# A mixer's decay table and one-hot rows, zero-filled from 48 to 128 rows

## The chip, the cores and the metric

The kernel runs on one core of a Trainium2 chip (trn2). The metric is the device time of one execution in microseconds. The time before is the median of three runs.

## The reference, cut to what matters

One layer of a hybrid network over 128 context tokens and 2,048 latent tokens of width 1,024, in chunks of 128 tokens. The part that the change touches is the decay between two tokens of one chunk in the state-space scan, for 8 heads and two directions:

```python
def ssd_chunked_scan(x, dt, a, bm, cm, h0):
    ...
    a_cum = jnp.cumsum((dt * a).reshape(b, nc, CHUNK, G, R), axis=2)
    ...
    lower = jnp.tril(jnp.ones((CHUNK, CHUNK), bool))[None, None, :, :, None, None]
    seg = a_cum[:, :, :, None] - a_cum[:, :, None, :]
    decay_in = jnp.exp(jnp.where(lower, seg, -jnp.inf))
    cb = jnp.einsum('bclgn,bcsgn->bclsg', cc, bc)
    y_diag = jnp.einsum('bclsgr,bcsgrp->bclgrp', cb[..., None] * decay_in, X)
```

Around it stand norms, the input projection, a depthwise convolution, pooling, the output projection, an expert-choice feed-forward layer with 16 experts, and a last norm.

## The kernel before

Tokens are split into 17 tiles of 128 (`NT` = 17; the first is the context). The program is a row of stages, each a block in which all engines have their own instruction stream, with a barrier at its end: `front` (input projection, convolution, pooling), `decays`, `back_states`, `mixer`, `selection`, `experts`, `final`.

`decays` makes the table of step sizes and cumulated decays `tab`, and a second copy of the cumulated decays, turned so that tokens lie along the columns: `acum_t`, 48 rows by 2,176 bf16 columns. Its 48 rows (`N3`) are 16 (8 heads in two directions, `HH`) times 3: an f32 value is split into three bf16 parts (`stack`, lines 1058 to 1062). VectorE does the softplus in a chain of dependent operations (lines 1032 to 1048), TensorE sums over tokens (1011 to 1013), VectorE splits, TensorE turns (1019), and ScalarE copies the result into `acum_t` (998, 999). Beside it GpSimd fills and selects constants (966 to 978): the triangles of minus infinity `negf` and `negb`, a bf16 identity, and `pick`, 48 rows by 16 x 128 columns, which holds for each of the 16 heads-and-directions ones in the three rows of that head. The selects wait for all fills (line 970).

`mixer` reads both. For each tile, `decay_rows` (TensorE) builds four quads of masks, two by two, in two PSUM banks `b34`. A quad is one product of the identity with a triangle over 512 columns (line 1351, all 128 rows) and, added on top, four products of `pick` with the tile's columns of `acum_t` (line 1354, 48 rows, 128 columns each). ScalarE takes the exponential of each quad (1517), VectorE adds the two directions (1609) and multiplies with the chunk's C-B products (1616), and TensorE's `scan` multiplies with the tokens (1385). The order of TensorE's work is written out by hand: for tile i `scan`, `route` of tile i-3 (1463), quads 0 and 1 of tile i+1, `turn_rows` (1453), half a projection of tile i-1 (`project`, 1441, 24 products), `turn_rows` again, quads 2 and 3 of tile i+1, `turn` of tile i+1 (1364 to 1375), the other half of the projection, `turn_y` (1425). Each step waits on counters of the engines that feed it.

Inputs of products that have to be exact are split in two f32r parts; their weight loads have 128 rows and 128 columns. The experts' stage gathers tokens in blocks of 128, 128 and 16 rows (`L2087` turns them).

Of the kernel before, what the change touches and what calls it, by code (L numbers as in the profile page):

```python
# [24 lines left out]
BF16 = mybir.dt.bfloat16  # L25
# [3 lines left out]
ACT = mybir.ActivationFunctionType  # L29
AX_X = mybir.AxisListType.X  # L30

P = 128
# [3 lines left out]
T = CTX + LAT  # L36
# [5 lines left out]
HH = 2 * H  # L42
# [13 lines left out]
R_DTB, R_ALOG, R_DSKIP, R_EDGE = 0, 16, 32, 40  # L56
# [884 lines left out]
def decays(nc, g, io):  # L941

    with ExitStack() as ctx:
# [7 lines left out]
        ps_row = k.ps("ps_row", [P, 2, D])  # L951
        made = k.sem("masks_made")
        dch = k.sem("decay_chain")
        mag_done, exp_done, aexp_done = k.sem("mag_done"), k.sem("spexp_done"), k.sem("aexp_done")
        lndt_done = k.sem("lndt_done")
        da_done, sums_done, acum_done, exps_done = k.sem("da_done"), k.sem("sums_done"), k.sem("acum_done"), k.sem("exps_done")
        row_done, row_copied = k.sem("row_done"), k.sem("row_copied")
        stack_done, acum_turned = k.sem("stack_done"), k.sem("acum_turned")
        tab = g.tab
        rows = [(g.mod[:, G_A:G_A + 8, w], g.ga_rows[:, w, :]) for w in range(2)]  # L960
# [3 lines left out]
        @block.gpsimd  # L964
        def _(pool):
            pool.memset(g.negf[:, :], 0.0).then_inc(made, 1)
            pool.memset(g.negb[:, :], 0.0).then_inc(made, 1)
            pool.tensor_copy(g.identb[:, :], g.ident[:, :]).then_inc(made, 1)
            pool.memset(g.pick[:, :, :], 0.0).then_inc(made, 1)
            pool.wait_ge(made, 4)  # L970

            pool.affine_select(out=g.negf[:, :], in_=g.negf[:, :], compare_op=ALU.is_ge, fill=NEG, base=0,
                               pattern=[[1, P]], channel_multiplier=-1)
            pool.affine_select(out=g.negb[:, :], in_=g.negb[:, :], compare_op=ALU.is_ge, fill=NEG, base=0,
                               pattern=[[-1, P]], channel_multiplier=1)
            for n in range(3):
                pool.affine_select(out=g.pick[:, :, :], in_=g.pick[:, :, :], compare_op=ALU.not_equal, fill=1.0,
                                   base=-HH * n, pattern=[[-1, HH], [0, P]], channel_multiplier=1).then_inc(made, 1)
                pool.wait_ge(made, 5 + n)

        @block.scalar
        def _(act):
            act.preload_act_table_set("natural_log_exp_and_others")
            act.activation(aexp[:, :], g.rows[:, R_ALOG:R_ALOG + HH], ACT.Exp).then_inc(aexp_done, 1)
            act.wait_ge(mag_done, 1)
            act.activation(e[:, :, :], mag[:, :, :], ACT.Exp, scale=-1.0).then_inc(exp_done, 1)
            for n, (_, dst) in enumerate(rows):
                act.wait_ge(row_done, n + 1)
                act.activation(dst, ps_row[:, n % 2, :], ACT.Copy).then_inc(row_copied, 1)
            act.wait_ge(da_done, 1)  # L990
            act.activation(z[:, :, :], tab[:, :, T_DT:T_DT + HH], ACT.Ln).then_inc(lndt_done, 1)
            act.wait_ge(acum_done, 1)

            act.activation(tab[:, :, T_EACUM:T_EACUM + HH], v[:, :, :], ACT.Exp).then_inc(exps_done, 1)
            act.activation(mag[:, :, :], mag[:, :, :], ACT.Exp).then_inc(exps_done, 1)
            act.activation(tab[:, :, T_DEC:T_DEC + HH], ps_tot[:, :, :], ACT.Exp).then_inc(exps_done, 1)
            act.wait_ge(acum_turned, 1)
            act.activation(g.acum_t[:, 0:T - P], ps_acum[0:N3, 0:T - P], ACT.Copy)
            act.activation(g.acum_t[:, T - P:T], ps_f[0:N3, :, :].rearrange("p t h -> p (t h)")[:, 0:P], ACT.Copy)

        @block.tensor
        def _(pe):
            for n, (col, _) in enumerate(rows):
                if n >= 2:
                    pe.wait_ge(row_copied, n - 1)
                for kk in range(KD):
                    mm = pe.matmul(ps_row[:, n % 2, P * kk:P * kk + P], col[:, kk:kk + 1].broadcast_to([P, P]),
                                   g.ident[:, :], start=True, stop=True)
                mm.then_inc(row_done, 1)
            pe.wait_ge(da_done, 1)  # L1010
            pe.matmul(ps_f[:, :, :], g.tri_le[:, :], tab[:, :, T_DA:T_DA + H], start=True, stop=True)
            pe.matmul(ps_b[:, :, :], g.tri_ge[:, :], tab[:, :, T_DA + H:T_DA + HH], start=True, stop=True)
            pe.matmul(ps_tot[:, :, :], g.ones[:, :], tab[:, :, T_DA:T_DA + HH], start=True, stop=True).then_inc(sums_done, 1)
            pe.wait_ge(made, 3)
            pe.wait_ge(row_copied, 2)
            pe.wait_ge(stack_done, 1)
            for i in range(NT):
                out = ps_acum[0:N3, P * i:P * i + P] if i < NT - 1 else ps_f[0:N3, :, :].rearrange("p t h -> p (t h)")[:, 0:P]
                mm = pe.matmul(out, stack[:, i, :], g.identb[:, :], start=True, stop=True)
            mm.then_inc(acum_turned, 1)  # L1020

        @block.vector
        def _(dve):
            count = [0]

            def link(ins):
                count[0] += 1
                ins.then_inc(dch, 1)
                dve.wait_ge(dch, count[0])

            bias = g.rows[:, R_DTB:R_DTB + HH].unsqueeze(1).broadcast_to([P, NT, HH])
            link(dve.tensor_tensor(v[:, :, :], g.dt_raw[:, :, :], bias, ALU.add))
            dve.scalar_tensor_tensor(mag[:, :, :], v[:, :, :], -1.0, v[:, :, :], ALU.mult, ALU.max).then_inc(mag_done, 1)
            link(dve.tensor_scalar(relu[:, :, :], v[:, :, :], 0.0, None, ALU.max))
            dve.wait_ge(exp_done, 1)

            link(dve.tensor_scalar(z2[:, :, :], e[:, :, :], 2.0, None, ALU.add))
            link(dve.reciprocal(poly[:, :, :], z2[:, :, :]))
            link(dve.tensor_tensor(z[:, :, :], e[:, :, :], poly[:, :, :], ALU.mult))
            link(dve.tensor_tensor(z2[:, :, :], z[:, :, :], z[:, :, :], ALU.mult))  # L1040
            link(dve.tensor_scalar(poly[:, :, :], z2[:, :, :], 1.0 / 17, None, ALU.mult))
            for n in (15, 13, 11, 9, 7, 5, 3):
                link(dve.scalar_tensor_tensor(poly[:, :, :], poly[:, :, :], 1.0 / n, z2[:, :, :], ALU.add, ALU.mult))
            link(dve.scalar_tensor_tensor(poly[:, :, :], poly[:, :, :], 1.0, z[:, :, :], ALU.add, ALU.mult))
            link(dve.scalar_tensor_tensor(tab[:, :, T_DT:T_DT + HH], poly[:, :, :], 2.0, relu[:, :, :], ALU.mult, ALU.add))
            dve.wait_ge(aexp_done, 1)
            aneg = aexp[:, :].unsqueeze(1).broadcast_to([P, NT, HH])
            dve.scalar_tensor_tensor(tab[:, :, T_DA:T_DA + HH], tab[:, :, T_DT:T_DT + HH], -1.0, aneg,
                                     ALU.mult, ALU.mult).then_inc(da_done, 1)
            dve.wait_ge(da_done, 1)  # L1050
            dve.wait_ge(sums_done, 1)
            dve.tensor_copy(v[:, :, 0:H], ps_f[:, :, :])
            link(dve.tensor_copy(v[:, :, H:HH], ps_b[:, :, :]))
            dve.wait_ge(lndt_done, 1)
            dve.tensor_tensor(mag[:, :, :], ps_tot[:, :, :], v[:, :, :], ALU.subtract).then_inc(acum_done, 1)
            dve.tensor_tensor(tab[:, :, T_NACUM:T_NACUM + HH], z[:, :, :], v[:, :, :], ALU.subtract)

            link(dve.tensor_copy(stack[:, :, 0:HH], v[:, :, :]))
            link(dve.tensor_tensor(rest[:, :, :], v[:, :, :], stack[:, :, 0:HH], ALU.subtract))
            link(dve.tensor_copy(stack[:, :, HH:2 * HH], rest[:, :, :]))  # L1060
            link(dve.tensor_tensor(rest[:, :, :], rest[:, :, :], stack[:, :, HH:2 * HH], ALU.subtract))
            dve.tensor_copy(stack[:, :, 2 * HH:N3], rest[:, :, :]).then_inc(stack_done, 1)
            dve.wait_ge(exps_done, 2)
            dve.tensor_tensor(tab[:, :, T_WEND:T_WEND + HH], mag[:, :, :], tab[:, :, T_DT:T_DT + HH], ALU.mult)


# [1345 lines left out]
def build(nc, io):  # L2412
    Kit.used.clear()
    with ExitStack() as ctx:
# [17 lines left out]
        with ExitStack() as part:  # L2432
# [2 lines left out]
            g.negf, g.negb = kk.sb("negf", [P, P], BF16), kk.sb("negb", [P, P], BF16)  # L2435
            g.identb = kk.sb("identb", [P, P], BF16)
            g.ga_rows = kk.sb("ga_rows", [P, 2, D])
            g.pick, g.acum_t = kk.sb("pick", [N3, HH, P], BF16), kk.sb("acum_t", [N3, T], BF16)
            g.wohi, g.wolo = kk.sb("wohi", [P, KD, D], F32R), kk.sb("wolo", [P, KD, D], F32R)
            g.wrs = kk.sb("wrs", [P, 2, KD, STRIP])  # L2440
            g.hf = kk.sb("hf", [P, 2, 512])
# [54 lines left out]
```

## Time and profile before

| | before |
|---|---|
| median of the runs | 2522.24 us |
| runs | 2519.30, 2522.86, 2522.24 us |
| the profiled execution | 2521.52 us |
| its span, first to last instruction | 2519.9 us |
| granted TensorE clock, mean | 0.938 |
| TensorE busy | 2261.8 us, 90% |
| VectorE busy | 1381.2 us, 55% |
| ScalarE busy | 998.2 us, 40% |
| GpSimd busy | 238.3 us, 9% |

One execution is profiled; the times of single instructions come from it. PE is TensorE's products, PEld its weight loads, DVE VectorE, ACT ScalarE, POOL GpSimd. The granted clock is a share of full speed: 1.00 is the level of 2.4 GHz and 0.50 that of 1.2 GHz. A product's recorded length is from its start to the end of its last column, and products overlap, so the distance between two starts says what one costs in a row of them, not its length.

### The profile page before, as it was taken

To read this page: it belongs to the slowest core of one execution; us is meant where nothing else is said; L and a number is where in the kernel's file an instruction comes from. 1 tells how busy PE (TensorE), PEld (TensorE's weight loads), DVE (VectorE), ACT (ScalarE), POOL (GpSimd) and SP (SyncE) were. 2 spreads that over 40 slices of the span, in tenths; PEclk is the share of its full clock that TensorE was granted. 3 is DMA by queue.
4 is the path that set the end of the run, shared out by engine and by line. 5 is a ranking of instruction groups with operands and counts; after the bars stand their busy time and mean duration, and the time that the engine had idled before them with its cause. 6 is when DMAs were issued, how large, how long until landed. Compare 5 with 4: busy or idle time off the path is not lost. (4 is left out here: it accounts for less than half of the span.)

```text
span 2519.9 us, 40046 instructions
## 1 busy us (share of the span) xinstructions
PE 2261.8 (90%) x15772; PEld 2052.0 (81%) x15772; DVE 1381.2 (55%) x2184; ACT 998.2 (40%) x1734; POOL 238.3 (9%) x307
## 2 busy tenths in 40 slices
PE   4999999956799999629999999999999999999980
PEld 2878887855688887518999999999999999999980
DVE  2655443226477777464566456655565555645543
ACT  3642222222455554104444444444444344434424
POOL 0000000021111111000100111101010110011010
PEclk8999999987799999758999999999999999999995
DMA  8533442216344443033665565656565655556537
GB/s 277 180 114 120 144 144 96 88 60 223 91 138 138 139 139 117 34 118 103 192 195 167 176 193 177 200 160 187 176 209 154 183 181 188 173 176 188 176 94 285
DMA packets 318699, 396.57 MB, mean 157 GB/s; under 512 B 12014, under 2 KB 273150, under 8 KB 316558
## 3 DMA queue, kind: packets, MB, share of 16 engines
q1 hardware_dynamic: 287406, 287.67, 35.7%
q0 software_dynamic: 22400, 86.06, 11.7%
q10 hardware_dynamic: 8800, 21.56, 2.3%
q8 instruction: 62, 1.02, 0.2%
q14 instruction: 31, 0.25, 0.0%
HBM read 318.12 MB, written 77.14 MB: 157 GB/s over the span
## 5 line engine op out<-in xcount | busy, mean ns | idle before, releaser
L2227 DVE TENSOR_TENSOR experts_wlo<-experts_raw,experts_whi 128x2048 fp32r<-128x2048 f32 x192 | 439.9, 2291 | 421.8 <-ACT experts_whi L2171 421.8
L2109 PE MATMUL experts_ps_r<-experts_xhi,experts_whi 128*128 128x272 f32 x2048 | 605.2, 296 | 5.4 <-DVE experts_xlo L2281 5.4
L2109 PE MATMUL experts_ps_r<-experts_xhi,experts_wlo 128*128 128x272 f32 x2048 | 593.8, 290 | 0.0
L2109 PE MATMUL experts_ps_r<-experts_xlo,experts_whi 128*128 128x272 f32 x2048 | 590.5, 288 | 0.0
L2109 PEld LDWEIGHTS experts_ps_r<-experts_xhi,experts_whi 128*128 128x128 f32 x2048 | 386.1, 189 | 8.5 <-DVE experts_xlo L2281 5.5
L2109 PEld LDWEIGHTS experts_ps_r<-experts_xlo,experts_whi 128*128 128x128 f32 x2048 | 386.9, 189 | 0.0
L2109 PEld LDWEIGHTS experts_ps_r<-experts_xhi,experts_wlo 128*128 128x128 f32 x2048 | 386.1, 189 | 0.0
L2171 ACT ACTIVATE experts_whi<-experts_raw 128x2048 fp32r<-128x2048 f32 x192 | 366.1, 1907 | 14.6 <-DMA experts_raw<-in_w_gate 13.8
L2109 PE MATMUL experts_ps_r<-experts_hhi,experts_whi 128*128 128x272 f32 x1024 | 299.6, 293 | 0.2 <-DVE experts_hlo L2301 0.2
L2109 PE MATMUL experts_ps_r<-experts_hhi,experts_wlo 128*128 128x272 f32 x1024 | 296.3, 289 | 0.0
L2109 PE MATMUL experts_ps_r<-experts_hlo,experts_whi 128*128 128x272 f32 x1024 | 294.8, 288 | 0.0
L521 PE MATMUL front_ps<-front_hhi,front_whi 128*128 128x384 f32 (+1 forms) x640 | 236.1, 369 | 0.0
L521 PE MATMUL front_ps<-front_hhi,front_wlo 128*128 128x384 f32 (+1 forms) x640 | 230.8, 361 | 0.0
L521 PE MATMUL front_ps<-front_hlo,front_whi 128*128 128x384 f32 (+1 forms) x640 | 230.8, 361 | 0.0
L2195 ACT ACTIVATE experts_hhi<-experts_hid 128x272 fp32r<-128x272 f32 x128 | 55.2, 431 | 353.9 <-DVE experts_hid L2298 353.9
L2109 PEld LDWEIGHTS experts_ps_r<-experts_hhi,experts_whi 128*128 128x128 f32 x1024 | 192.7, 188 | 1.1 <-DVE experts_hlo L2301 0.5
L2109 PEld LDWEIGHTS experts_ps_r<-experts_hlo,experts_whi 128*128 128x128 f32 x1024 | 193.0, 188 | 0.0
L2109 PEld LDWEIGHTS experts_ps_r<-experts_hhi,experts_wlo 128*128 128x128 f32 x1024 | 192.6, 188 | 0.0
L521 PEld LDWEIGHTS front_ps<-front_hhi,front_whi 128*128 128x128 f32 x640 | 120.8, 189 | 25.4 <-ACT front_u L659 12.6
L659 ACT ACTIVATE front_u<-front_ps 128x128 f32<-128x128 f32 (+2 forms) x90 | 40.2, 469 | 248.9 <-PE front_ps L521 227.9
L2049 POOL DMA_INDIRECT x<-experts_yo,experts_idx x48 | 72.1, 1502 | 684.1 <-DVE experts_yo L2288 521.1
L2190 ACT ACTIVATE experts_sg<-experts_ps_r 128x272 f32<-128x272 f32 x128 | 51.0, 398 | 214.9 <-PE experts_ps_r L2109 214.9
(393 smaller groups left out, 3453.5 us busy)
## 6 DMA issues: line engine op xcount, KB each, us to landing
experts_raw<-in_w_gate SPq DMA_DIRECT2D x64, 1024.0 KB, 5.0
experts_raw<-in_w_up SPq DMA_DIRECT2D x64, 1024.0 KB, 5.0
experts_raw<-in_w_down SPq DMA_DIRECT2D x64, 1024.0 KB, 5.3
shared_whalf<-in_w_ada SPq DMA_DIRECT2D x16, 1024.0 KB, 5.2
mixer_mz<-mixed SPq DMA_DIRECT2D x17, 768.0 KB, 7.9
mixed<-front_acc POOLq DMA_DIRECT2D x9, 1024.0 KB, 4.2
resid<-early_xin POOLq DMA_DIRECT2D x17, 512.0 KB, 3.7
mixer_xs<-resid SPq DMA_DIRECT2D x17, 512.0 KB, 4.0
```

Source lines behind the costliest of these rows:

```text
L521: mm = pe.matmul(ps[:, out, 0:n], wt[buf][:, kk, :], h[:, kk, t0:t0 + n], start=(kk == 0 and q == 0), stop=(kk == KD - 1 and q == 2))
L659: ins = act.activation(dst_u[:, uo:uo + pn], ps[:, bank_of(s), po:po + pn], func)
L2049: pool.indirect_dma_start(io["x2"], bass.IndirectOffsetOnAxis(idx[2][0:n, a:a + 1], 0), yo[0:n, a, :], None, compute_op=ALU.add).then_inc( ...
L2109: mm = pe.matmul(dst, w[:, c % RING, kk, cols], r[:, kk, :], start=(kk == 0 and q == 0), stop=(kk == KD - 1 and q == 2))
L2171: act.activation(whi[:, c % RING, :, :], raw[:, c % RAW, :, :], ACT.Copy).then_inc(whi_done, 1)
L2190: act.activation(sg[:, ft % 2, :], ps_r[:, (2 * ft) % 4, 0:ROWS], ACT.Silu).then_inc(silu_done, 1)
L2195: act.activation(hhi[:, ft, :], hid[:, ft % 2, :], ACT.Copy).then_inc(hhi_done, 1)
L2227: dve.tensor_tensor(wlo[:, c % RING, :, :], raw[:, c % RAW, :, :], whi[:, c % RING, :, :].bitcast(F32), ALU.subtract).then_inc(wlo_done, 1)
```

## The change

`pick` and `acum_t` get 128 rows instead of 48. Rows 48 to 127 hold zeros: `pick`'s come from its fill, which now covers 128 rows, and `acum_t` gets a fill of its own on GpSimd, as the fifth, so that all thresholds of `made` behind it move by one. The products of line 1354 then read 128 rows of both; no line of the mixer changes. ScalarE's copies into `acum_t` are confined to rows 0 to 47 and wait for the fill. Five semaphores that ScalarE raised (`exp_done`, `aexp_done`, `lndt_done`, `exps_done`, `row_copied`) become one counter, `scalar_done`, on which the others wait with thresholds, and a branch that was never taken goes.

```diff
-        mag_done, exp_done, aexp_done = k.sem("mag_done"), k.sem("spexp_done"), k.sem("aexp_done")
-        lndt_done = k.sem("lndt_done")
...
+        mag_done, scalar_done = k.sem("mag_done"), k.sem("scalar_done")
+        A_RATE, A_EXP, A_ROWS, A_LN, A_DECAYS = 1, 2, 4, 5, 7
...
             pool.memset(g.pick[:, :, :], 0.0).then_inc(made, 1)
-            pool.wait_ge(made, 4)
+            pool.memset(g.acum_t[:, :], 0.0).then_inc(made, 1)
+            pool.wait_ge(made, 5)
...
-                pool.wait_ge(made, 5 + n)
+                pool.wait_ge(made, 6 + n)
...
-            act.activation(aexp[:, :], g.rows[:, R_ALOG:R_ALOG + HH], ACT.Exp).then_inc(aexp_done, 1)
+            act.activation(aexp[:, :], g.rows[:, R_ALOG:R_ALOG + HH], ACT.Exp).then_inc(scalar_done, 1)
...
+            act.wait_ge(made, 5)
             act.wait_ge(acum_turned, 1)
-            act.activation(g.acum_t[:, 0:T - P], ps_acum[0:N3, 0:T - P], ACT.Copy)
-            act.activation(g.acum_t[:, T - P:T], ps_f[0:N3, :, :].rearrange("p t h -> p (t h)")[:, 0:P], ACT.Copy)
+            act.activation(g.acum_t[0:N3, 0:T - P], ps_acum[0:N3, 0:T - P], ACT.Copy)
+            act.activation(g.acum_t[0:N3, T - P:T], ps_f[0:N3, :, :].rearrange("p t h -> p (t h)")[:, 0:P], ACT.Copy)
...
             pe.wait_ge(made, 3)
-            pe.wait_ge(row_copied, 2)
+            pe.wait_ge(scalar_done, A_ROWS)
...
-            dve.wait_ge(exp_done, 1)
+            dve.wait_ge(scalar_done, A_EXP)
...
-            dve.wait_ge(aexp_done, 1)
+            dve.wait_ge(scalar_done, A_RATE)
...
-            dve.wait_ge(lndt_done, 1)
+            dve.wait_ge(scalar_done, A_LN)
...
-            dve.wait_ge(exps_done, 2)
+            dve.wait_ge(scalar_done, A_DECAYS)
...
-            g.pick, g.acum_t = kk.sb("pick", [N3, HH, P], BF16), kk.sb("acum_t", [N3, T], BF16)
+            g.pick, g.acum_t = kk.sb("pick", [P, HH, P], BF16), kk.sb("acum_t", [P, T], BF16)
```

## Rows read from the trace of the kernel before

**Rows 1.** The page: granted TensorE clock in 40 equal slices, in tenths.

```profile
PEclk8999999987799999758999999999999999999995
```

**Rows 2.** Stretches: length, busy us (instructions) by engine, granted clock, DMA share, GB/s.

```profile
660.00:680.00 20.00, 16.55 (x68) 13.85 (x69) 11.70 (x19) 9.96 (x33) 3.09 (x3) 0.60 0.14 40
...
691.76:992.96 301.20, 301.20 (x1919) 241.94 (x1918) 221.82 (x365) 160.56 (x503) 38.11 (x42) 1.00 0.42 135
```

**Rows 3.** TensorE's products in order of time: start, length in us, line, out<-in.

```profile
781.80 0.64 PE L1463 MATMUL mixer_b<-mixer_h2t,ssd_wrs 128*32 128x128 f32 x16
782.37 0.39 PE L1351 MATMUL mixer_b<-ssd_negf,ssd_identb 128*128 128x512 bf16 x1
782.70 0.39 PE L1354 MATMUL mixer_b<-ssd_acum_t,ssd_pick 48*128 48x128 bf16 x4
783.02 0.39 PE L1351 MATMUL mixer_b<-ssd_negf,ssd_identb 128*128 128x512 bf16 x1
...
783.67 0.66 PE L1453 MATMUL mixer_b<-kept_ident,mixer_xr 128*128 128x128 f32 x4
...
789.64 0.60 PE L1453 MATMUL mixer_b<-kept_ident,mixer_xr 128*128 128x128 f32 x4
790.08 0.38 PE L1351 MATMUL mixer_b<-ssd_negb,ssd_identb 128*128 128x512 bf16 x1
...
792.88 0.48 PE L1441 MATMUL mixer_b<-ssd_wohi,mixer_mhi 128*128 128x512 f32 x1
...
798.90 1.90 PE L1385 MATMUL mixer_b<-mixer_xt,mixer_ex 128*128 128x64 f32 x16
```

**Rows 4.** TensorE's weight loads in order of time, with the idle time before.

```profile
782.69 0.22 PEld L1354 LDWEIGHTS mixer_b<-ssd_acum_t,ssd_pick 48*128 48x128 bf16 x4 [0.23 <-issue]
...
789.97 0.10 PEld L1351 LDWEIGHTS mixer_b<-ssd_negb,ssd_identb 128*128 128x128 bf16 x1
```

**Rows 5.** Groups, 691.76 to 992.96: count | busy us, mean ns | idle before.

```profile
L1354 PE MATMUL mixer_b<-ssd_acum_t,ssd_pick 48*128 48x128 bf16 x224 | 22.1, 219 | 0.0
...
L1354 PEld LDWEIGHTS mixer_b<-ssd_acum_t,ssd_pick 48*128 48x128 bf16 x224 | 12.4, 94 | 14.2 <-issue 14.2
```

**Rows 6.** Groups of weight loads in the experts, 1300 to 1420, by shape.

```profile
L2087 PEld LDWEIGHTS experts_ps_x<-kept_ident,experts_xg 128*128 128x128 f32 x24 | 2.9, 141 | 0.7 <-issue 0.7
...
L2087 PEld LDWEIGHTS experts_ps_x<-kept_ident,experts_xg 16*128 16x128 f32 x12 | 1.6, 133 | 2.0 <-issue 2.0
```

**Rows 7.** VectorE in order of time, in the same tile.

```profile
778.35 1.23 DVE L1695 TENSOR_TENSOR mixer_xr<-mixer_o,mixer_xs 128x1024 f32<-128x1024 f32 x1
...
790.28 0.69 DVE L1672 COPY mixer_h2t<-mixer_b 128x512 f32<-128x512 f32 x1 [1.84 <-PE mixer_b L1453]
...
795.68 1.21 DVE L1616 TENSOR_TENSOR mixer_ex<-mixer_ex,mixer_cbt 128x1024 f32<-128x1024 f32 x1
```

**Rows 8.** GpSimd in order of time, decays and the start of the next stage.

```profile
539.71 1.79 POOL L969 MEMSET ssd_pick<- 48x2048 bf16 x1
...
542.20 6.32 POOL L977 TENSOR_SCALAR_AFFINE_SELECT ssd_pick<-ssd_pick 48x2048 bf16<-48x2048 bf16 x3
563.84 0.53 POOL L1102 MEMSET ssd_wrs<- 128x512 f32 x1 [15.32 <-SPq L1118]
```

**Rows 9.** VectorE in order of time, decays.

```profile
540.00 1.66 DVE L1034 TENSOR_SCALAR decays_sp_relu<-decays_sp_v 128x272 f32<-128x272 f32 x1
541.70 0.40 DVE L1037 TENSOR_SCALAR decays_sp_z<-decays_sp_e 128x272 f32<-128x272 f32 x1
...
546.69 1.98 DVE L1041 TENSOR_SCALAR decays_sp_poly<-decays_sp_z 128x272 f32<-128x272 f32 x1
548.71 3.30 DVE L1043 SCALAR_TENSOR_TENSOR decays_sp_poly<-decays_sp_poly,decays_sp_z 128x272 f32<-128x272 f32 x7
```

**Rows 10.** ScalarE in order of time, end of decays.

```profile
561.50 1.87 ACT L998 ACTIVATE ssd_acum_t<-decays_ps_row 48x2048 bf16<-48x2048 f32 x1 [3.68 <-PE decays_ps_f L1019]
```

**Rows 11.** TensorE's products in order of time, before the experts' first tile.

```profile
1113.25 1.02 PE L2075 MATMUL experts_ps_i<-experts_val_e,experts_onehot 128*128 128x5 bf16 x32 [5.24 <-DVE experts_onehot L2239]
```

More of the change, by code:

```diff
@@ L953, in decays @@
         dch = k.sem("decay_chain")
-        mag_done, exp_done, aexp_done = k.sem("mag_done"), k.sem("spexp_done"), k.sem("aexp_done")
-        lndt_done = k.sem("lndt_done")
-        da_done, sums_done, acum_done, exps_done = k.sem("da_done"), k.sem("sums_done"), k.sem("acum_done"), k.sem("exps_done")
-        row_done, row_copied = k.sem("row_done"), k.sem("row_copied")
+        mag_done, scalar_done = k.sem("mag_done"), k.sem("scalar_done")
+        A_RATE, A_EXP, A_ROWS, A_LN, A_DECAYS = 1, 2, 4, 5, 7
+        da_done, sums_done, acum_done = k.sem("da_done"), k.sem("sums_done"), k.sem("acum_done")
+        row_done = k.sem("row_done")
         stack_done, acum_turned = k.sem("stack_done"), k.sem("acum_turned")
@@ L983, in _ @@
             act.preload_act_table_set("natural_log_exp_and_others")
-            act.activation(aexp[:, :], g.rows[:, R_ALOG:R_ALOG + HH], ACT.Exp).then_inc(aexp_done, 1)
+            act.activation(aexp[:, :], g.rows[:, R_ALOG:R_ALOG + HH], ACT.Exp).then_inc(scalar_done, 1)
             act.wait_ge(mag_done, 1)
-            act.activation(e[:, :, :], mag[:, :, :], ACT.Exp, scale=-1.0).then_inc(exp_done, 1)
+            act.activation(e[:, :, :], mag[:, :, :], ACT.Exp, scale=-1.0).then_inc(scalar_done, 1)
             for n, (_, dst) in enumerate(rows):
                 act.wait_ge(row_done, n + 1)
-                act.activation(dst, ps_row[:, n % 2, :], ACT.Copy).then_inc(row_copied, 1)
+                act.activation(dst, ps_row[:, n % 2, :], ACT.Copy).then_inc(scalar_done, 1)
             act.wait_ge(da_done, 1)
-            act.activation(z[:, :, :], tab[:, :, T_DT:T_DT + HH], ACT.Ln).then_inc(lndt_done, 1)
+            act.activation(z[:, :, :], tab[:, :, T_DT:T_DT + HH], ACT.Ln).then_inc(scalar_done, 1)
             act.wait_ge(acum_done, 1)
-            act.activation(tab[:, :, T_EACUM:T_EACUM + HH], v[:, :, :], ACT.Exp).then_inc(exps_done, 1)
-            act.activation(mag[:, :, :], mag[:, :, :], ACT.Exp).then_inc(exps_done, 1)
-            act.activation(tab[:, :, T_DEC:T_DEC + HH], ps_tot[:, :, :], ACT.Exp).then_inc(exps_done, 1)
+            act.activation(tab[:, :, T_EACUM:T_EACUM + HH], v[:, :, :], ACT.Exp).then_inc(scalar_done, 1)
+            act.activation(mag[:, :, :], mag[:, :, :], ACT.Exp).then_inc(scalar_done, 1)
+            act.activation(tab[:, :, T_DEC:T_DEC + HH], ps_tot[:, :, :], ACT.Exp).then_inc(scalar_done, 1)
+            act.wait_ge(made, 5)
             act.wait_ge(acum_turned, 1)
-            act.activation(g.acum_t[:, 0:T - P], ps_acum[0:N3, 0:T - P], ACT.Copy)
-            act.activation(g.acum_t[:, T - P:T], ps_f[0:N3, :, :].rearrange("p t h -> p (t h)")[:, 0:P], ACT.Copy)
+            act.activation(g.acum_t[0:N3, 0:T - P], ps_acum[0:N3, 0:T - P], ACT.Copy)
+            act.activation(g.acum_t[0:N3, T - P:T], ps_f[0:N3, :, :].rearrange("p t h -> p (t h)")[:, 0:P], ACT.Copy)
         @block.tensor
@@ L1003, in _ @@
             for n, (col, _) in enumerate(rows):
-                if n >= 2:
-                    pe.wait_ge(row_copied, n - 1)
                 for kk in range(KD):
```

## The prediction

> **What bounds the kernel now.** I read the page's strip of forty slices first: TensorE is at full clock nearly everywhere, with dips in slices 9 to 11 and 17 to 19 [rows 1]. The edit touches two stages. The preparation of the decays lies at 539 to 564 us, the mixer at 634.8 to about 1040 us, and the two tensors that grow are read in the mixer alone. The second view is the busy time by stretch [rows 2]: from 691.76 to 992.96 us, which is fourteen whole tiles of the mixer (21.5 us each), TensorE is busy for 301.20 of 301.20 us at granted clock 1.00; VectorE has 221.82, ScalarE 160.56 us. So TensorE sets the pace there by itself, and what it is spared comes off the end if nobody else becomes late. Before that, at 660 to 680 us, the granted clock averages 0.60 and TensorE is busy for 16.55 of 20 us: the first two tiles are not of this kind.
>
> The third view is TensorE in order of time inside one tile [rows 3]. A tile issues four "quads" of decay masks: one 512-column product that writes the triangle of minus infinity (line 1351, all 128 rows) and four 128-column products that add the decays (line 1354, 48 rows). At 782.37 the first quad starts, at 783.02 the second, at 783.67 what follows: 0.65 us each. A quad streams 1,024 columns, which at one column a cycle of the 2.4 GHz level is 0.43 us. The four mask products last 0.39 together and one alone 219 ns [rows 5], so their pitch is (0.39 - 0.22)/3 = 0.057 us, and a quad at that pitch is 0.455. Hence 0.20 to 0.22 us of each quad is not streaming. Where: from the 512-column product to the first mask product 0.33 (0.21 to 0.23 is streaming, so 0.10 to 0.12 lost), and the rest behind the last mask product.
>
> The weight loads say why [rows 4]. The load for the full-row product at 789.97 starts while the f32 products of 789.64 still run: it is pulled ahead, and 790.08 is just 4 x 0.11 behind 789.64. The load for the first 48-row product at 782.69 starts only when the product before it has streamed out, marked by 0.23 us of idle. So it is neither the change of type (f32 to bf16 costs nothing at 790.08) nor of column count, but going from 128 rows to 48 and back. The expert stage has the same pattern with another size [rows 6]: 24 loads of 128 x 128 had 0.7 us of idle before them in all, 12 loads of 16 x 128 had 2.0, or 0.17 each.
>
> **The change part by part.** (a) Rows 48 to 127 of the one-hot rows and of the decay table become zeros that are multiplied; the product is the same. Number and columns of products stay. Loads take 94 ns with 48 rows [rows 5] and 0.10 us with 128 [rows 4], so nothing is added per product. What goes is the two switches per quad. I take 0.205 us, between 0.195 (pitch 0.057) and 0.22 (2.4 GHz columns). Behind a quad an f32 load of 128 rows comes twice per tile; it might hide less well than a bf16 load, but today the first f32 group behind a quad already takes 0.66 instead of 0.60 [rows 3], so I leave this at nothing, +-0.05. Quads for tiles 2 to 16 run in the stretch that TensorE bounds: 15 x 4 = 60, 60 x 0.205 = 12.3 us. Tile 0's four are at the half-speed level, and half of them stand before the exponentials that tile 0 waits for: 0 to 0.8, taken 0.2. Tile 1's four are followed by idle time: 0.
>
> On this the Trainium skill has two rules that disagree. "TensorE: Matmul & The Clock Gate" (LDWEIGHTS) says that a load's time depends on its columns and not on the contraction rows; by that alone the padding is worth nothing, and the sum would be the cost of part (b) only. "TensorEngine Tiling (Array Packing)" (Key Properties) says that changing the tiling mode drains the engine; by that all 0.2 us per quad goes. Rows 3 and 4 agree with both: equal loads, but a stall where the row count changes.
>
> Is there room for 12 us? At the end of a tile, three VectorE results are what TensorE takes next [rows 3, 7]: the residual ends at 778.35 + 1.23 = 779.58 for the product at 781.80 (2.2 us spare); the copied rows at 790.28 + 0.69 = 790.97 for the projection at 792.88 (1.9; the two quads in front save 0.4 of it); the masked product at 795.68 + 1.21 = 796.89 for 798.90 (2.0, no quad lies between). A tile loses only 0.8, so nothing turns late. Tile period: 21.56 to 20.74.
>
> (b) GpSimd gets one more fill, 128 x 2176 bf16, behind the 48 x 2048 one that took 1.79 us at 539.71 [rows 8]. The fill of 512 f32 columns over 128 rows took 0.53, so rows don't price it and columns do: (1.79 - 0.53)/1536 = 0.82 ns each, hence 1.79 + 128 x 0.82 ns = 1.90. It delays the five selects behind it, which ended at 542.20 + 6.32 = 548.52. Nobody waits on GpSimd's semaphores before 561.5; still it isn't hidden. VectorE's operations stretch while GpSimd works [rows 9]: a tensor_scalar that takes 0.40 at 541.70 took 1.66 at 540.00 and 1.98 at 546.69, each ending 0.15 us behind a GpSimd operation, and the run of unstretched ones starts at 548.71, right behind GpSimd's last. With the fill, the last select ends at 550.4 and that run starts about 550.6: +1.85. VectorE's chain feeds the sums, the table and ScalarE's copy into it at 561.50 [rows 10], after which the next stage starts (563.84), so all of it is on the path. Bounds: 1.4, if one more short operation slips in between two fills, and 1.95; nothing below 1.4 as the selects themselves can't start before the fill ends.
>
> "SBUF — State Buffer" of the Trainium skill (Who interferes with whom) describes an exclusive lock on a port pair shared by VectorE and GpSimd, held for a whole instruction; rows 8 and 9 agree for the tensor_scalar operations.
>
> (c) Semaphores merged into one counter of ScalarE: its operations end in order, and the thresholds 1, 2, 4, 5, 7 stand behind the same operations as the old semaphores. The wait of the table's copy on the fifth fill is met about 18 us earlier. Both 0. (d) 80 more partitions in two tensors: same bytes per partition, 0.
>
> Sum: -12.3 - 0.2 + 1.85 = -10.65 us. On the profiled execution (2521.52, of which 2519.9 span) that is 2510.9; the median shown is 0.72 above it, 2522.24, and gives **2511.6**.
>
> **The rivals.** *Rows don't matter:* the gap is due to the change in columns or in accumulate flags, and padding leaves it. Gain 0, cost 1.85: 2524.1. Against it: 790.08 in rows 3. *One switch only:* the gap behind the quads stays, say because of their semaphore. Then 60 x 0.105 = 6.3 goes: 2517.8. Against it: the f32 products before 790.08 signal too, without a gap. *A new wait:* VectorE's mask sum or the exponentials turn late and give back part of the 0.8 per tile; needs 2.0 us of slack to be gone; with half given back 2517.8 too. *Slower:* full-row loads can't be pulled ahead of a full-row product that is running, so the three mask products behind the first of a quad each expose some 0.09 us; 180 x 0.09 = 16.2, no switch gain, +1.85: 2540.3. It decides from 0.06 us per product. "TensorE: Matmul & The Clock Gate" of the Trainium skill (Part 3, The mechanism) does say that loads overlap running products only when the row group differs. Against it are 32 full-row bf16 products of 5 columns in 1.02 us, (1.02 - 0.17)/31 = 0.027 apart [rows 11], and the pulled-ahead load of 789.97. *Clock edge:* the clock came back at about 676 us, in tile 1's products [rows 2]; everything reaches this place some 1.7 us later. If the edge stays where it is in time, 1.7 us less of that work runs at half speed (0.85 gained); if it comes as much later again, 0.85 are lost, and twice that with two such edges. This widens the others.
>
> **How the numbers follow.** Forecast 2511.6, 0.79, its own range 2507.5 to 2515.5 (gain per quad 0.19 to 0.22 gives +-1, (b) +-0.4, clock and the spread of the runs shown, 3.6 us, the rest). One switch or a new wait 0.10 at 2517.8. No gain 0.09 at 2524.1. Slower 0.02 at 2540.3. What a measurement can tell from no change is 0.2%, 5.0 us: below 2517.2 is faster, above 2527.3 slower. Faster: 0.79 and half of the 0.10, 0.84; slower 0.02; same 0.14. Range 2507.5 to 2518.5: it takes in the forecast's and most of the 2517.8 cases and leaves out the rest.
>
> **What would show it.** In the changed profile: 60 quads of about 0.44 us, the load of the first mask product starting with the 512-column product still running; tile period 20.7; TensorE still without a wait; the run of seven operations of line 1043 starting at 550.6; the mixer starting 1.85 later. Wrong if the first load of a quad still has 0.2 us of idle before it, if a wait on ScalarE or VectorE shows up in front of line 1385, or if the mask products' pitch grows over 0.06.

## The result and the profile after

Four runs of the changed kernel gave a median of 2505.88 us (2503.95 to 2508.14), beside 2522.55 for the kernel before (also four runs): ratio 0.9936, 95% interval 0.9919 to 0.9953. It is faster, by 16.7 us where 10.65 were forecast, and lies below the range, whose lower end was 2507.5. Two later sets of runs, on which more below, gave 0.9959 and 0.9958, that is 10 to 11 us. So two things are to be explained: what the change is worth, and why the first figure said more.

The profiled execution after took 2508.14 us, its span is 2506.6 against 2519.9. The counterpart of [rows 2] comes first: the fourteen whole tiles, from the tile's first product of line 1385 to the fifteenth, at full clock in both kernels.

```profile
688.37:976.65 288.28, 288.28 (x1919) 242.30 (x1917) 221.76 (x365) 160.56 (x503) 38.09 (x42) 1.00 0.44 141
```

288.28 us instead of 301.20: 12.92 less, 0.92 a tile, at the same number of products. TensorE is still busy without a gap, and VectorE (221.76) and ScalarE (160.56) do what they did: nobody became late.

TensorE in order of time inside one tile, products and then weight loads (start, length, line), the counterpart of [rows 3] and [rows 4]:

```profile
774.72 0.65 PE L1463 MATMUL mixer_b<-mixer_h2t,ssd_wrs 128*32 128x128 f32 x16
775.30 0.39 PE L1351 MATMUL mixer_b<-ssd_negf,ssd_identb 128*128 128x512 bf16 x1
775.52 0.39 PE L1354 MATMUL mixer_b<-ssd_acum_t,ssd_pick 128*128 128x128 bf16 x4
775.75 0.38 PE L1351 MATMUL mixer_b<-ssd_negf,ssd_identb 128*128 128x512 bf16 x1
775.96 0.39 PE L1354 MATMUL mixer_b<-ssd_acum_t,ssd_pick 128*128 128x128 bf16 x4
776.19 0.61 PE L1453 MATMUL mixer_b<-kept_ident,mixer_xr 128*128 128x128 f32 x4
776.55 0.47 PE L1441 MATMUL mixer_b<-ssd_wohi,mixer_mhi 128*128 128x512 f32 x1
```

```profile
775.29 0.10 PEld L1351 LDWEIGHTS mixer_b<-ssd_negf,ssd_identb 128*128 128x128 bf16 x1 [0.20 <-issue]
775.31 0.43 PEld L1354 LDWEIGHTS mixer_b<-ssd_acum_t,ssd_pick 128*128 128x128 bf16 x4
775.69 0.10 PEld L1351 LDWEIGHTS mixer_b<-ssd_negf,ssd_identb 128*128 128x128 bf16 x1
...
776.13 0.42 PEld L1453 LDWEIGHTS mixer_b<-kept_ident,mixer_xr 128*128 128x128 f32 x4
```

A quad now lasts 775.75 - 775.30 = 0.45 and 0.44 us, where it lasted 0.65. The load for the first mask product starts at 775.31, 0.01 behind the start of the 512-column product, and no longer after it has streamed out. The f32 group behind the second quad passes the array on after 0.36 us (776.19 to 776.55); before, it took 0.41 (783.67 to 784.08):

```profile
784.08 0.48 PE L1441 MATMUL mixer_b<-ssd_wohi,mixer_mhi 128*128 128x512 f32 x1
```

One idle of 0.20 us is left, in front of the first quad's load at 775.29, and it was there before as well:

```profile
781.79 0.38 PEld L1463 LDWEIGHTS mixer_b<-mixer_h2t,ssd_wrs 128*32 128x32 f32 x16 [0.33 <-issue]
782.37 0.10 PEld L1351 LDWEIGHTS mixer_b<-ssd_negf,ssd_identb 128*128 128x128 bf16 x1 [0.20 <-issue]
```

It does not belong to the 48 rows. It comes behind `route` (line 1463), whose weights have 128 rows but only 32 columns, and the first of those loads has 0.33 us of idle in front of it. So narrow weights show the same sign as few rows. The change leaves these two gaps as they are, and no run here tests what they cost.

The other stage, decays, shows the price. GpSimd, then VectorE, the counterparts of [rows 8] and [rows 9]:

```profile
537.22 1.79 POOL L969 MEMSET ssd_pick<- 128x2048 bf16 x1
538.96 1.90 POOL L970 MEMSET ssd_acum_t<- 128x2176 bf16 x1
...
541.56 6.32 POOL L978 TENSOR_SCALAR_AFFINE_SELECT ssd_pick<-ssd_pick 128x2048 bf16<-128x2048 bf16 x3
```

```profile
537.51 3.51 DVE L1034 TENSOR_SCALAR decays_sp_relu<-decays_sp_v 128x272 f32<-128x272 f32 x1
541.05 0.40 DVE L1037 TENSOR_SCALAR decays_sp_z<-decays_sp_e 128x272 f32<-128x272 f32 x1
...
543.89 2.12 DVE L1040 TENSOR_TENSOR decays_sp_z<-decays_sp_z 128x272 f32<-128x272 f32 x1
...
548.07 2.35 DVE L1043 SCALAR_TENSOR_TENSOR decays_sp_poly<-decays_sp_poly,decays_sp_z 128x272 f32<-128x272 f32 x5
```

The fill takes 1.90 us as estimated, and the tensor_scalar of line 1034, which takes 0.39 undisturbed (`pick_later`, below) and had been stretched to 1.66, is stretched to 3.51: it waits for both fills. The tensor_tensor at 543.89 takes 2.12 beside a select, as it did in the kernel before (with no select beside it, it takes 0.44, as the run `pick_later` shows below):

```profile
544.53 2.12 DVE L1040 TENSOR_TENSOR decays_sp_z<-decays_sp_z 128x272 f32<-128x272 f32 x1
```

Stage lengths of the profiled executions, each from the stage's first instruction to the next stage's first, in us ("whole tiles" is one tile's mean over the fourteen):

```
kernel            front   decays  back    mixer   select  experts  final  whole tile
before            539.13  24.66   70.96   407.01  67.62   1357.34  53.19  21.51
before_again      538.68  24.65   70.80   406.87  67.64   1354.42  55.73  21.51
sem_only          537.51  24.64   71.35   407.61  67.63   1358.91  54.04  21.51
fill_only         536.51  26.67   68.64   407.03  67.60   1360.71  54.79  21.51
rows64            536.99  26.57   69.49   405.79  67.77   1358.49  53.61  21.51
grouped           540.46  24.65   69.17   400.94  67.71   1356.39  54.22  21.09
rows96            537.84  26.57   70.30   393.32  67.01   1357.92  54.31  20.60
after             536.65  26.57   70.68   392.58  66.34   1360.14  53.61  20.59
after_again       538.17  26.58   67.91   393.45  67.65   1357.33  53.08  20.59
after_third       538.98  26.57   69.87   393.17  66.97   1357.84  54.79  20.59
fill_late         536.76  24.72   72.26   393.01  67.01   1355.61  52.52  20.59
pick_later        537.93  19.73   69.89   393.13  67.60   1359.40  53.59  20.59
pick_later_again  538.14  20.59   69.96   393.55  67.72   1358.14  51.05  20.59
```

(Most whole tiles last 21.56 and 20.64; the first of the fourteen is 0.7 shorter, as `route` has no work there yet.) Three columns follow the edits: the whole tile to 0.01 us; decays to 0.1, but for the last two rows, on which more below; the mixer within 1 to 2 us. Front, back_states, the experts and final wander by 4, 4, 6 and 5 us, whatever the kernel.

### The profile page after: what moved, and what is told of

It is laid out like the page before. It is cut to its first block and busy times, and to the rows that moved or that the text cites. A ratio compares the mean times of both kernels' runs of the same rounds, so it can differ in the third digit from the quotient of the medians.

```text
span 2506.6 us, 40048 instructions
## 1 busy us (share of the span) xinstructions
PE 2242.5 (89%) x15772; PEld 2049.5 (82%) x15772; DVE 1383.0 (55%) x2184; ACT 998.0 (40%) x1734; POOL 240.2 (10%) x308
## 3 DMA queue, kind: packets, MB, share of 16 engines
q0 software_dynamic: 22400, 86.06, 11.7%
q10 hardware_dynamic: 8800, 21.56, 2.3%
## 5 line engine op out<-in xcount | busy, mean ns | idle before, releaser
L2171 ACT ACTIVATE experts_whi<-experts_raw 128x2048 fp32r<-128x2048 f32 x192 | 366.1, 1907 | 14.6 <-DMA experts_raw<-in_w_gate 13.8
```

What stands on the lines that cost most here:

```text
L2171: act.activation(whi[:, c % RING, :, :], raw[:, c % RAW, :, :], ACT.Copy).then_inc(whi_done, 1)
```

## The experiments

**Is the size of the gain real?** The changed kernel again, and the kernel before against itself.

> The changed kernel once more, to size the gain. Theory A (the medians of four runs caught luck): the tile period and the stages say 13 us, so the ratio comes out at 0.9945 to 0.9950 (about 12 to 14 us). Theory B (something outside the stages that the two profiles compare): the ratio stays at 0.9935 (16 to 17 us), and a second profile shows the missing 3 us in one place, in front or in the experts.

> The kernel before against itself: ratio 1.000 with an interval of about 0.001. Its second profile shows how far the stages that the change does not touch move from run to run: the first profiles differ by 2.5 us in front (537.7 and 535.3) and by 2.8 the other way in the experts. If these are chance, the same size of difference appears here; if the change causes them, front lasts 537.7 +- 0.3 again.

`after_again`: 2506.98 us (8 runs) against 2519.02 (31 runs on the same chip), ratio 0.9959 (0.9943 to 0.9976). `before_again`: 1.0004 (0.9990 to 1.0018). In its profile the experts last 1354.42 us, 2.9 less than in the first profile of the same program, so a stage that nothing touches moves by that much. Front moved by only 0.5 there (538.68 against 539.13), which leaves its 2.5 us between the first two profiles undecided; the other rows of the table decide it: the changed kernel has 538.17 and 538.98 in its next two profiles, and kernels with 48 rows have 536.51 to 540.46. So they are no effect of the change. (The expectation counts front from a start 1.4 us later than the table.) As to the size, the ratio 0.9959 lies above theory A's 0.9945 to 0.9950, but its interval takes them in and leaves out theory B's 0.9935: theory A, with a gain at the small end.

> The changed kernel a third time. If the gain is the fourteen whole tiles and their edges, 13.8 to 14.4, less 1.9 for the fill, the ratio is 0.9950 +- 0.001 (12 to 12.5 us) as in the second set, and the 16.7 us of the first four runs were chance. If 16.7 is the true size, the ratio is at or under 0.994.

`after_third`: 2510.81 (5 runs) against 2520.90 (9), ratio 0.9958 (0.9945 to 0.9972): 10.1 us. Over all sets, the 17 runs of the changed kernel have a mean of 2507.95 (standard deviation 2.9), the 70 distinct runs of the kernel before 2519.69 (3.2): 11.7 us. With such a spread the mean of four runs is uncertain by 1.5 us, and the difference of two such means by 2.2; the first set was off by 5, over twice that. Chance makes so large a difference only rarely, and no run shows another reason.

**What is it about 48 rows?**

> The changed kernel with 64 rows instead of 128 in both tensors. Theory A (the array is switched to a mode of at most 64 rows and back): nothing is gained against 48 rows, tile period 21.56 us, two gaps of 0.10 per quad, total 2524. Theory B (what counts is a load whose rows end within a group of 32, as 48 do): 64 rows are enough, period 20.64, total as the changed kernel.

> The changed kernel with 96 rows. Theory A (mode of at most 64 rows, or full): 96 rows run in the full mode, period 20.64 us, total as the changed kernel (2506 to 2509). Theory B (any count other than the neighbour's 128 costs the gap): period 21.56, total 2524.

```diff
-            g.pick, g.acum_t = kk.sb("pick", [P, HH, P], BF16), kk.sb("acum_t", [P, T], BF16)
+            g.pick, g.acum_t = kk.sb("pick", [96, HH, P], BF16), kk.sb("acum_t", [96, T], BF16)
```

(64 in the other.) TensorE's products in order of time, first with 64 rows, then with 96:

```profile
779.98 0.39 PE L1351 MATMUL mixer_b<-ssd_negf,ssd_identb 128*128 128x512 bf16 x1
780.30 0.39 PE L1354 MATMUL mixer_b<-ssd_acum_t,ssd_pick 64*128 64x128 bf16 x4
780.63 0.39 PE L1351 MATMUL mixer_b<-ssd_negf,ssd_identb 128*128 128x512 bf16 x1
```

```profile
777.20 0.39 PE L1351 MATMUL mixer_b<-ssd_negf,ssd_identb 128*128 128x512 bf16 x1
777.42 0.39 PE L1354 MATMUL mixer_b<-ssd_acum_t,ssd_pick 96*128 96x128 bf16 x4
777.65 0.38 PE L1351 MATMUL mixer_b<-ssd_negf,ssd_identb 128*128 128x512 bf16 x1
```

0.65 us a quad with 64 rows, as with 48; 0.45 with 96, as with 128. The totals go along: 2521.12 against 2519.02, ratio 1.0016 (1.0003 to 1.0029), so 64 rows only cost; and 2507.88, ratio 0.9955 (0.9942 to 0.9969). It is not that some rows stay unused (96 leave 32), nor that 48 isn't a multiple of 32 (64 is). It fits an array that works in one mode at 48 and 64 rows and in another at 96 and 128, with the change of mode as what costs; the next experiment tests that second half. Theory A both times. This is the drain that "TensorEngine Tiling (Array Packing)" of the Trainium skill states under Key Properties, and its list of modes has a step at 64 rows and none between 64 and 128.

**Does the price hang on the number of changes of mode?**

> The kernel before (48 rows) with another order of TensorE's work: of each pair of quads, first both 512-column products, then all eight mask products. Same products, but two changes of the row count per pair instead of four. Theory A (each change of the array's mode costs 0.10 us): period 21.56 - 4 x 0.10 = 21.16 us, mixer some 6 us shorter, less about 1 us in the first tile, where the fourth quad waits for exponentials. Theory B (the gap belongs to what comes after a product of 512 columns, or to the mask products themselves): period stays at 21.56.

```diff
                 for q in quads:
...
                     pe.matmul(b34[:, q % 2, :], g.identb[:, :], neg[:, :].unsqueeze(1).broadcast_to([P, 4, P]),
                               start=True, stop=False, skip_group_check=True)
+                for q in quads:
                     for hh in range(4):
```

```profile
780.79 0.60 PE L1351 MATMUL mixer_b<-ssd_negf,ssd_identb 128*128 128x512 bf16 x2
781.33 0.62 PE L1355 MATMUL mixer_b<-ssd_acum_t,ssd_pick 48*128 48x128 bf16 x8
781.88 0.66 PE L1454 MATMUL mixer_b<-kept_ident,mixer_xr 128*128 128x128 f32 x4
```

A pair of quads takes 1.09 us (780.79 to 781.88) instead of 1.30, with the same products and two changes instead of four: 0.105 per change. Most tiles last 21.14 us, forecast 21.16. The kernel is at 2514.00 against 2521.22, ratio 0.9973 (0.9963 to 0.9982), and its mixer 6 us shorter: not quite half of the gain in the mixer (14), at no cost in fills. The first f32 group still takes 0.41 (781.88 to 782.29): that surplus belongs to the last change, from 48 back to 128.

**What does the fill cost, and why?**

> The kernel before with the new fill alone, over its 48 rows, and ScalarE's wait for it. If columns price a fill and not rows, decays lasts 26.57 us as with 128 rows; if rows count, between 24.66 and 25.5. Tile period 21.56.

> The merging of five semaphores alone, 48 rows and no new fill. Both theories: decays 24.66, tile period 21.56, nothing.

The first is the kernel before with

```diff
             pool.memset(g.pick[:, :, :], 0.0).then_inc(made, 1)
-            pool.wait_ge(made, 4)
+            pool.memset(g.acum_t[:, :], 0.0).then_inc(made, 1)
+            pool.wait_ge(made, 5)
...
-                pool.wait_ge(made, 5 + n)
+                pool.wait_ge(made, 6 + n)
...
+            act.wait_ge(made, 5)
             act.wait_ge(acum_turned, 1)
```

and the second the changed kernel with

```diff
-            g.pick, g.acum_t = kk.sb("pick", [P, HH, P], BF16), kk.sb("acum_t", [P, T], BF16)
+            g.pick, g.acum_t = kk.sb("pick", [N3, HH, P], BF16), kk.sb("acum_t", [N3, T], BF16)
```

and without the fill and its wait. `fill_only`: decays 26.67, whole tile unchanged. Columns price the fill. (One run each: 2523.56 and 2523.28 us, within the spread of the kernel before.) `sem_only`: decays 24.64, whole tile unchanged, nothing.

The price is the same in `fill_only`, but another operation pays it. GpSimd, then VectorE:

```profile
537.09 1.79 POOL L969 MEMSET ssd_pick<- 48x2048 bf16 x1
538.83 2.06 POOL L970 MEMSET ssd_acum_t<- 48x2176 bf16 x1
```

```profile
537.38 1.66 DVE L1036 TENSOR_SCALAR decays_sp_relu<-decays_sp_v 128x272 f32<-128x272 f32 x1
539.07 1.97 DVE L1039 TENSOR_SCALAR decays_sp_z<-decays_sp_e 128x272 f32<-128x272 f32 x1
```

Here the first tensor_scalar got in behind the first fill (it ended at 539.04) and the second one waited out the second fill, where in the changed kernel one operation waited out both (3.51). What decides between the two is not shown. The first fill took 1.79 over 48 rows as over 128. The second took 2.06 instead of 1.90; it was recorded from 538.83 on, while the tensor_scalar was still there, so its extra 0.16 may be that overlap and not the rows.

> The changed kernel with the new fill moved behind the three selects on GpSimd; ScalarE's copy waits for it there. Theory A (the fill costs because it pushes the selects, and they hold up VectorE's short operations): decays takes 24.66 us again instead of 26.57, since the operations of line 1043 run beside a fill at their usual 0.44. Theory B (any GpSimd work holds VectorE up): the fill stretches one operation of line 1043 by 1.9 us, and decays stays at 26.57.

```diff
             pool.memset(g.pick[:, :, :], 0.0).then_inc(made, 1)
-            pool.memset(g.acum_t[:, :], 0.0).then_inc(made, 1)
-            pool.wait_ge(made, 5)
+            pool.wait_ge(made, 4)
...
-                pool.wait_ge(made, 6 + n)
+                pool.wait_ge(made, 5 + n)
+            pool.memset(g.acum_t[:, :], 0.0).then_inc(made, 1)
+            pool.wait_ge(made, 8)
...
-            act.wait_ge(made, 5)
+            act.wait_ge(made, 8)
```

Its GpSimd and VectorE in order of time:

```profile
546.20 1.95 POOL L980 MEMSET ssd_acum_t<- 128x2176 bf16 x1
546.33 3.30 DVE L1044 SCALAR_TENSOR_TENSOR decays_sp_poly<-decays_sp_poly,decays_sp_z 128x272 f32<-128x272 f32 x7
```

The seven operations take 3.30 us beside the fill as they took without it [rows 9], and decays is back at 24.72. So a fill holds up a tensor_scalar and not these operations with two inputs, and theory A's time is right. Its wording is too narrow: in the changed kernel the fill both pushed the selects by 1.9 us and held up the tensor_scalar of line 1034 itself. That agrees with "SBUF — State Buffer" of the Trainium skill (Who interferes with whom), by which an operation with two inputs in SBUF meets only GpSimd work that reads SBUF. The total, 2505.30 (4 runs), ratio 0.9937 (0.9917 to 0.9958), can't tell 1.85 us; the stage can.

**All of GpSimd's work out of VectorE's way.**

> The changed kernel with GpSimd's work kept away from VectorE's chain: the one-hot rows are built in the next stage, where GpSimd waits for 9 us anyway, and the table's fill starts behind the seventh step of the chain. If the selects stretch VectorE by 1.25 + 1.6 + 1.6 us and the fill by 1.9, decays lasts 20.7 us against 26.57, nothing else changes, and the kernel is 5.9 us faster than the changed one. Rival: the building costs the next stage as much (its VectorE operation at line 1199 meets the selects), sum 0 to 2.

```diff
-            pool.memset(g.pick[:, :, :], 0.0).then_inc(made, 1)
-            pool.memset(g.acum_t[:, :], 0.0).then_inc(made, 1)
-            pool.wait_ge(made, 5)
+            pool.wait_ge(made, 3)
...
+            pool.wait_ge(dch, 7)
+            pool.memset(g.acum_t[:, :], 0.0).then_inc(made, 1)
...
-            act.wait_ge(made, 5)
+            act.wait_ge(made, 4)
...
             pool.memset(g.wrs[:, :, :, :], 0.0).then_inc(wr_zero, 1)
+            pool.memset(g.pick[:, :, :], 0.0).then_inc(pick_made, 1)
+            for n in range(3):
+                pool.wait_ge(pick_made, n + 1)
+                pool.affine_select(out=g.pick[:, :, :], in_=g.pick[:, :, :], compare_op=ALU.not_equal, fill=1.0,
+                                   base=-HH * n, pattern=[[-1, HH], [0, P]], channel_multiplier=1).then_inc(pick_made, 1)
```

VectorE in decays, in order of time:

```profile
538.80 0.39 DVE L1030 TENSOR_SCALAR decays_sp_relu<-decays_sp_v 128x272 f32<-128x272 f32 x1
...
542.56 0.44 DVE L1036 TENSOR_TENSOR decays_sp_z<-decays_sp_z 128x272 f32<-128x272 f32 x1
543.04 0.30 DVE L1037 TENSOR_SCALAR decays_sp_poly<-decays_sp_z 128x272 f32<-128x272 f32 x1
```

The operations that had taken 1.66 to 3.51, 2.12 and 1.98 take 0.39, 0.44 and 0.30. Decays lasts 19.73 us, 6.8 less than in the changed kernel, and back_states 69.89, inside its usual 68 to 72. That range is too wide to rule the rival out; the trace does it. VectorE in back_states:

```profile
561.29 1.18 DVE L1202 TENSOR_TENSOR ssd_wrs<-back_states_wr,kept_scale_m 128x128 f32<-128x128 f32 x2 [7.80 <-DMA back_states_wr<-in_w_router]
574.00 0.69 DVE L1215 TENSOR_TENSOR back_states_xw<-back_states_ps_x,ssd_tab 128x512 f32<-128x512 f32 x1 [11.53 <-PE back_states_ps_b L1155]
```

The two products that meet the selects take 1.18 us, where they take 0.49 in the changed kernel, but VectorE then waits 11.53 us for TensorE, so these 0.7 us are nobody's loss. The total is 2500.71 against 2521.22 (6 runs), ratio 0.9925 (0.9907 to 0.9943).

> The kernel with the one-hot rows built a stage later, again, beside the changed kernel on one chip. Its decays stage is 6.8 us shorter than the changed kernel's in the trace; if nothing is given back, it is faster than the changed one by 6.8 us (0.27%), if the next stage gives it back, by 4 or less.

Ratio 0.9914 (0.9901 to 0.9928), 2499.72 against the changed kernel's 2510.81 on the same chip. That is 11.1, more than the stage explains; over both sets it is 2500.9 (11 runs) against 2507.95, 7.0 us, which is the stage's 6.8 or 6.0. Decays lasted 20.59 here: VectorE waited 2.34 us for TensorE's sums instead of 1.48, as their products fell into a stretch with granted clock 0.50 where the other run had 0.84. The changed kernel also waited 2.34 us at granted clock 0.50, so 20.59 is the one to compare with its 26.57: 6.0 less, forecast 5.9. (The 20.7 of the first expectation does not follow from its own terms, which give 26.57 - 6.35 = 20.2.) This version beats both kernels, by some 19 and 7 us.

## Why the prediction missed

**What bounds the mixer, and what a quad loses: right.** The forecast was a tile of 20.74 us instead of 21.56; most tiles last 20.64. A quad lost 0.20 (0.65 to 0.445), forecast 0.205. The cause, going from 128 rows to 48 and back, is shown by three experiments (64, 96, grouped), and no wait took the place of the stall: TensorE is busy for all of the fourteen tiles, so the slack of about 2 us at [rows 3, 7] was enough. One sign that the prediction had named for being wrong did turn up, 0.20 us of idle before the first load of a quad. It stands behind the 32-column weights of line 1463 in both kernels; the prediction had not looked at that change.

**The term that was mis-sized** is in part (a): "I leave this at nothing, +-0.05". The f32 group behind a quad does get shorter, by 0.05 us twice a tile, as the last change of mode also delayed that group's first product. The row that says so was there, 0.66 against 0.60 [rows 3], and I used it to cancel a loss that doesn't exist. Product by product, one tile against another: quads 0.81, f32 groups 0.10, the rest 0.03; the mean over the fourteen tiles is 0.92. Over 15 tiles (the fourteen, and tile 2's quads, which are made one tile earlier) the term is 13.8 instead of 12.3. With the fill, 1.91 measured and 1.85 forecast, the sum comes to some -12 instead of -10.65, and the 11.7 us over all runs agree with it. A misreading in part (b) cost nothing: TensorE does wait on GpSimd's counter before 561.5, ahead of its product of 559.49, but for the third count, which was there 20 us earlier.

**The tiles before and behind the fourteen.** The mixer got shorter by 13.4 to 14.4 us in the three profiles of the changed kernel, and the fourteen tiles by 12.9 in each. The rest, 0.5 to 1.5, is a difference of two parts. The stretch ahead of the fourteen tiles lasts 57.01 us before and 54.49, 56.08 and 55.47 after, which holds 0.9 for the quads of tile 2; the stretch behind them lasts 48.81 before and 49.82, 49.10 and 49.43 after, so it got longer. TensorE is not at full clock in either. The first pair, each stretch of the kernel before and then of the changed one:

```profile
634.75:691.76 57.01, 48.88 (x227) 37.70 (x228) 27.12 (x40) 24.56 (x77) 6.40 (x6) 0.70 0.32 93
992.96:1041.77 48.81, 35.61 (x218) 27.81 (x216) 21.65 (x40) 12.89 (x35) 3.27 (x7) 0.89 0.20 76
633.88:688.37 54.49, 43.08 (x227) 34.84 (x227) 27.12 (x40) 24.52 (x77) 6.37 (x6) 0.81 0.33 97
976.65:1026.47 49.82, 36.82 (x218) 28.36 (x216) 21.64 (x40) 12.89 (x35) 3.28 (x7) 0.87 0.20 74
```

The granted clock rose from 0.70 to 0.81 in the first stretch (in 660 to 680 us it was 0.83 after and 0.60 before [rows 2]) and fell from 0.89 to 0.87 in the last. The prediction gave such edges +-0.85 to 1.7 at the start of the mixer and nothing at its end; the size is about right, how much of it is the clock is not shown.

**The range.** The step that failed there is "clock and the spread of the runs shown". I took a spread from three runs, 3.6 us, and gave it a part of +-4 us together with the clock, as if the median to come were known to 1 or 2 us. The same program runs from 2510.6 to 2526.3. The median shown, 2522.24, itself stood 2.5 above the mean of 70 runs, and the four runs of the changed kernel 2 below the mean of 17. These two make the other 4 to 5 us between 12 and 16.7, and as far as the runs show they are luck: which few runs were drawn, not what the change does. So the miss of 5.7 us is 1 to 1.5 of mis-sized terms and the rest a range too narrow for medians of three and four runs. Which stage makes a run short or long I can only narrow: front, back_states, the experts and final carry the differences between profiles; what sets them from run to run stays open.

**The rivals.** "Rows don't matter" is refuted by 96 rows, "one switch only" by the gap that went on both sides of the mask products, "slower" by the loads that start 0.01 us behind a running full-row product, "a new wait" by 288.28 busy of 288.28.

## What to carry to other kernels

A group of products with few rows (48 and 64 here) between full-row ones costs two changes of mode, about 0.1 us each, that no busy share shows: look for weight loads that don't start with the product before them. Pad the rows (96 was enough here), or put such products in a row; it pays where TensorE sets the pace. Weights of few columns (32 here) show the same idle time and are worth the same look, though no run here tried them. And GpSimd work that is on nobody's path can still stretch VectorE's short operations: place it beside operations that don't mind it, or in a stage where VectorE waits.

## What the runs showed of the hardware

- 48 and 64 rows behave alike, and so do 96 and 128. Each change between the two kinds costs 0.10 to 0.11 us at full clock, and an f32 group behind one another 0.05.
- A load behind 32-column weights has 0.20 us of idle before it, and the first 32-column load behind 128-column weights 0.33, in both kernels.
- A VectorE tensor_scalar of 0.39 us waited out two GpSimd fills in a row (3.51 us) in the changed kernel; in `fill_only` it got in between them (1.66), and the next one waited out the second (1.97). A scalar_tensor_tensor with two inputs runs beside such a fill at its usual 0.44; a tensor_tensor of 0.44 is stretched to 2.12 beside a select.
- A fill of 2,176 bf16 columns takes 1.90 to 1.95 us over 128 rows and took 2.06 over 48, where it overlapped a tensor_scalar; one of 2,048 columns takes 1.79 over either.
- The same program varies from 2510.6 to 2526.3 us between executions, with a standard deviation of 3.2, while single stages repeat to 0.1 us (decays) and whole tiles to 0.01.
